# Bringing four rows of slots and weights to all partitions by way of DRAM instead of by products and evictions

## The reference

```python
def hier_moe(h, w_group, b_group, w_router, b_router, w_gate, w_up, w_down):
    """Two-level MoE: top-1 expert group, then top-2 experts inside that group."""
    ...
    top_v, top_i = lax.top_k(el_g, TOP_K_IN_GROUP)
    p_e = jax.nn.softmax(top_v, axis=-1) * p_g
    eidx = top_g[:, None] * EXP_PER_GROUP + top_i
    gates = (jax.nn.one_hot(eidx, N_EXPERTS, dtype=f32) * p_e[..., None]).sum(1).astype(x.dtype)
    y = jnp.zeros_like(x)
    for grp in range(N_GROUPS):
        sl = slice(grp * EXP_PER_GROUP, (grp + 1) * EXP_PER_GROUP)
        hg = jnp.einsum('td,edf->tef', x, w_gate[sl])
        hu = jnp.einsum('td,edf->tef', x, w_up[sl])
        act = jax.nn.silu(hg) * hu * gates[:, sl, None]
        y = y + jnp.einsum('tef,efd->td', act, w_down[sl])
```

## Time and profile before

| | us |
|---|---|
| median of 3 runs | 608.97 |
| lowest and highest | 608.93, 609.97 |
| the profiled execution, its own time | 609.4 |
| its span in the profile | 607.5 |
| mean granted clock of TensorE | 0.997 of full speed |

### The profile page before, as it was taken

One profiled execution on the slowest core, in us unless ns is written; L12 is line 12 of the kernel. 1 busy time (PEld: TensorE's weight loads), 2 busy tenths in 40 slices (PEclk: granted clock), 3 DMA queues, 4 the chain that ended last, 5 costly groups with the idle time before them and its releaser, 6 DMA issues.

```text
span 607.5 us, 8074 instructions
## 1 busy us (share of the span) xinstructions
PE 590.3 (97%) x3093; PEld 368.2 (61%) x3093; DVE 214.8 (35%) x625; ACT 146.6 (24%) x408; POOL 42.6 (7%) x87
## 2 busy tenths in 40 slices
PE   8999999999999999999998999999999899999996
PEld 4687878887664444444466777777777633333331
DVE  3352113420255444444464333333411542222222
ACT  3313123331321111111163333333311421111110
POOL 7010000000020000000003000000000111000000
PEclk9999999999999999999999999999999999999998
DMA  9979620126547999999997523120327598999971
GB/s 286 343 190 349 221 91 1 64 76 237 197 129 304 415 410 421 421 421 372 349 349 245 174 69 141 54 86 1 138 70 276 209 376 329 413 421 421 421 318 71
DMA packets 59124, 150.05 MB, mean 247 GB/s; under 512 B 10092, under 2 KB 42924, under 8 KB 46796
## 3 DMA queue, kind: packets, MB, share of 16 engines
q1 hardware_dynamic: 54992, 138.75, 61.2%
q0 software_dynamic: 2912, 10.64, 5.0%
q10 hardware_dynamic: 1180, 0.12, 0.2%
HBM read 146.27 MB, written 3.23 MB: 246 GB/s over the span
## 4 chain that ended last, share of the span: by engine, by line
PE 90%; DMA 5%; DVE 2%; ACT 1%; issue 1%; SPq 0%; DVEq 0%; POOLq 0%; ACTq 0%
PE bank L1395 36%; PE bank L1676 19%; PE bank L1704 9%; PE bank L1718 5%; PE bank L1647 3%; PE bank L1723 3%; PE bank L1506 1%; DMA qk_area<-xs,idx 1%; DMA ring<-in_m_w_in 1%; PE bank L1845 1%; PE bank L1889 1%; PE bank L1858 1%; PE bank L1885 1%; PE bank L1683 1%; DMA gate_area<-cs_dram 1%
## 5 line engine op out<-in xcount | busy, mean ns | idle before, releaser
L1395 PE MATMUL bank<-hxT,ring 128*128 128x272 f32 x576 | 138.2, 394 | 0.6 <-DVEq L1319 0.5
L1395 PEld LDWEIGHTS bank<-hxT,ring 128*128 128x128 f32 x576 | 107.8, 190 | 23.1 <-issue 2.1
L1676 PE MATMUL bank<-ring,gate_area 128*64 128x512 f32 x496 | 115.1, 597 | 0.0
L1676 PEld LDWEIGHTS bank<-ring,gate_area 128*64 128x64 f32 x496 | 34.5, 137 | 63.4 <-issue 62.6
L1395 PE MATMUL bank<-tok,ring 128*128 128x272 f32 (+1 forms) x256 | 59.6, 389 | 0.7 <-DVE tok L1372 0.6
L1704 PE MATMUL bank<-ring,gate_area 128*32 128x512 f32 (+1 forms) x368 | 58.0, 594 | 0.0
L1395 PEld LDWEIGHTS bank<-tok,ring 128*128 128x128 f32 x256 | 47.8, 190 | 11.8 <-issue 3.9
L1107 DVE TENSOR_TENSOR qk_area<-qk_area,bank 128x256 f32<-128x256 f32 x16 | 6.7, 422 | 92.6 <-ACT qk_area L754 92.6
L1704 PEld LDWEIGHTS bank<-ring,gate_area 128*32 128x32 f32 (+1 forms) x368 | 16.5, 119 | 36.2 <-issue 36.2
L538 POOL DMA_INDIRECT qk_area<-xs,idx x16 | 15.8, 987 | 311.7 <-DMA xs<-tok 199.4
L754 ACT ACTIVATE qk_area<-bank 128x256 f32<-128x256 f32 x16 | 6.2, 384 | 121.6 <-PE bank L1676 121.6
(11 more groups left out here) (302 smaller groups left out, 642.3 us busy)
## 6 DMA issues: line engine op xcount, KB each, us to landing
ring<-in_moe_w_gate SPq DMA_DIRECT2D x31, 1024.0 KB, 9.0
ring<-in_moe_w_up SPq DMA_DIRECT2D x31, 1024.0 KB, 10.8
ring<-in_moe_w_down SPq DMA_DIRECT2D x31, 1024.0 KB, 13.7
ring<-in_m_w_in SPq DMA_DIRECT2D x12, 1024.0 KB, 12.5
ring<-in_kv_w SPq DMA_DIRECT2D x8, 1024.0 KB, 12.4
ring<-in_m_w_out SPq DMA_DIRECT2D x4, 1024.0 KB, 12.9
ring<-in_f_w_q SPq DMA_DIRECT2D x4, 1024.0 KB, 12.0
ring<-in_f_w_o SPq DMA_DIRECT2D x4, 1024.0 KB, 6.6
```

Of the source, the lines that this page charges most:

```text
L1395: ins = pe.matmul(bank[c % 2][:, 0:n], w[:, k, half * P:half * P + P], x[:, k, 0:n], start=(k == 0), stop=(k == KB - 1))
L1676: ins = pe.matmul(bank[1][s, :], xgT[b % 2][:, q, s], unit_gate_up(us[par][0], q), start=(q == 0), stop=(q == KB - 1))
```

## The change

tokens_to_rows loses the second product of each tile. VectorE's copy to row4 takes 4 partitions instead of 36. ScalarE, behind xgT_evac(0) and ahead of silu(0), waits for row4 and issues a DMA that writes its four rows of n numbers to row4_dram. Where rows_spread made four evictions, ScalarE now waits for that write to have landed, and issues one DMA that reads the four rows back with a partition broadcast into bc4. combine_weights(0) waits for this DMA. The four products of spread_rows are gone, with their waits.

```diff
@@ build @@
+        row4_dram = nc.dram_tensor("row4_dram", [2, MH, NT], F32, kind="Internal").ap()
...
@@ LAYER0 @@
-                  1, "lg_read": 1, "bc_mm": 4, "bc_ready": 4, "xT_read": 8, ...
+                  1, "lg_read": 1, "bc_ready": 16, "xT_read": 8, ...
...
@@ ScalarE, moe(l) @@
                 def rows_spread():
 
-                    for r in range(4):
-                        act.wait_ge(*in_layer("bc_mm", l, r + 1))
-                        act.activation(bc4[:, r, 0:n], bank[4 + r][:, 0:n], ACT.Copy).then_inc(sem("bc_ready"), 1)
+                    act.wait_ge(sem("row4_out"), 16 * (l + 1))
+                    act.dma_start(bc4[:, :, 0:n], row4_dram[l, :, 0:n].partition_broadcast(P)).then_inc(sem("bc_ready"), 16)
...
                 xgT_evac(0)
+
+                act.wait_ge(*in_layer("row4_ready", l, 1))
+                act.dma_start(row4_dram[l, :, 0:n], row4[0:MH, 0:n]).then_inc(sem("row4_out"), 16)
                 for b in range(NPAIR):
                     silu(b)
...
@@ VectorE, moe(l) @@
                     if b == 0:
-                        dve.wait_ge(*in_layer("bc_ready", l, 4))
+                        dve.wait_ge(*in_layer("bc_ready", l, 16))
...
                 dve.wait_ge(*in_layer("row4_mm", l, 1))
-                dve.tensor_copy(row4[:, 0:n], bank[3][0:32 + MH, 0:n]).then_inc(sem("row4_ready"), 1)
+                dve.tensor_copy(row4[0:MH, 0:n], bank[3][0:MH, 0:n]).then_inc(sem("row4_ready"), 1)
...
@@ TensorE, moe(l) @@
                     for t, rows, c0 in tiles:
-                        pe.transpose(bank[3][0:MH, c0 - off:c0 - off + rows], tok4[0:rows, :, t], ident[0:rows, 0:rows])
-                        ins = pe.matmul(bank[3][32:32 + MH, c0 - off:c0 - off + rows], tok4[0:rows, :, t],
-                                        ident[0:rows, 0:rows], start=True, stop=True)
+                        ins = pe.transpose(bank[3][0:MH, c0 - off:c0 - off + rows], tok4[0:rows, :, t],
+                                           ident[0:rows, 0:rows])
                     ins.then_inc(sem("row4_mm"), 1)
-
-                def spread_rows(r0, r1):
-                    if r0 == 0:
-                        pe.wait_ge(*in_layer("row4_ready", l, 1))
-                        pe.wait_ge(*in_layer("xr_read", l, 1))
-                    for r in range(r0, r1):
-                        g = slice(32 * (r % 2), 32 * (r % 2) + MH)
-                        pe.matmul(bank[4 + r][:, 0:n], sel4[g, r, :], row4[g, 0:n], start=True, stop=True) \
-                            .then_inc(sem("bc_mm"), 1)
...
                     if b == 0:
                         rows_to_cols(1, 1)
-                        spread_rows(0, 2)
                         act_tr(0)
-                        spread_rows(2, 4)
                         continue
```

More of the change, by code:

```diff
@@ L284, in build @@
                   1, "rs_ffn": 1, "xr_tr": 6, "soft_in": 2, "soft_exp": 2, "xr_read":
-                  1, "lg_read": 1, "bc_mm": 4, "bc_ready": 4, "xT_read": 8, "xT_read0": 9, "gu_done": 8, "silu_done": 8,
+                  1, "lg_read": 1, "bc_ready": 16, "xT_read": 8, "xT_read0": 9, "gu_done": 8, "silu_done": 8,
                   "act_ready": 8, "down_done": 16, "y_read0": 8, "y_read1": 8, "eall_ready": 1, "pos_mm": 1,
```

## The result

| | before | after |
|---|---|---|
| median of 4 runs, us | 609.16 | 617.04 |
| lowest to highest, us | 608.93 to 609.97 | 616.64 to 617.5 |
| the profiled execution, us | 609.4 | 617.36 |

The ratio is 1.0127, 95% interval 1.0111 to 1.0143: 7.9 us slower. I had forecast 612.2 with a range up to 616.0. The direction was right, the size was not.

The account below looks back on a forecast made before the run. TensorE, busy for 97% of the span, was taken as the bound. Its gain of 2.1 us and late spreads of 1.8 and 3.5 us sum to +3.2, so 612.2 us after median adjustment, range 608.0 to 616.0.

Parts of the forecast that it names:

- Turning the tokens to rows, and the products: TensorE's path in both layers: removing L1618 and the four products gains 1.15 us in layer 0, 0.95 in layer 1.
- ScalarE costs nothing: ScalarE behind xgT_evac(1): the four evictions L738, 1.41 us, and the DMA issues in their place are worth nothing.
- Who waits: VectorE's combine_weights(0) waits for the rows; the idx copy behind it delays down(0). Allowed: 5.7 and 5.0 us to landing.
- Layer 0, 1.8 us late: Layer 0's spread: lands 7.5 us after issue against 5.7 allowed, so 1.8 us late, ends 0.6 and 3.3.
- Layer 1, 3.5 us late: Layer 1's spread: 512 packets land 8.5 us after issue, 3.5 us late, ends 0 and 6.0.
- the turns of one to one: DMA queues in layer 1: spread and loads alternate packet by packet; some 190 of 512 packets through until 504.3.
- rival D: DMA queues take turns in batches: layer 0 0.7 us late, layer 1 as forecast, 611.1 us; chance 0.10.
- rival E: TensorE's pause lowers its clock to 1.2 GHz: down(0) takes 3.65 us more in each layer, 619.5; chance 0.06.
- A: The forecast case, both layers' spreads late: 612.2 us, from 610.2 to 616.2 by the ends; chance 0.57.
- The sum: Whole kernel: -2.1 + 1.8 + 3.5 = +3.2 us on the profiled 609.4, so 612.6; forecast median 612.2.
- B: Both layers' spreads land in time, under 5.7 and 5.0 us: -2.1, 606.9 us; chance 0.15.
- C: Layer 0's spread in time, layer 1's late by about 2 us: 608.9, no change; chance 0.12.

Follow-up runs that it names:

- The last experiment: Changed kernel with layer 0's spread issued before silu(0), layer 1's in larger descriptors with its readers moved later: 608.58 us against 609.97 for the kernel before, ratio 0.9974.
- layer 0 alone: Changed kernel with only layer 0 spreading by DRAM, layer 1 keeping products and evictions: 610.05 us against 610.06 for the kernel before, ratio 1.0002.
- the larger descriptors: Changed kernel with layer 1's spread contiguous at both ends, 128 runs of 4 KB instead of 512 of 1 KB: 615.71 us, ratio 1.0096 to the kernel before.
- the kernel with the early issue: Changed kernel with the spread issued ahead of silu(0), once the write to DRAM has landed: 612.82 us against 609.71 for the kernel before, ratio 1.0052.

## Why the prediction was right and wrong

**Turning the tokens to rows, and the products.** Right. gate_up(1) starts 0.96 us earlier in layer 1 (forecast 0.95), and in layer 0 at 188.17 instead of 189.43; 0.13 of these 1.26 us the profile had gained earlier already, which leaves 1.13 (forecast 1.15). What was late next was VectorE's L1107 and L1114, as said. The last experiment shows most of the gain where nothing holds TensorE up behind it.

**ScalarE costs nothing.** Right for the engine. But the step that placed the issue was wrong: I let the queue issue the spread when ScalarE would have started its first L738, at 188.05 and 496.63. It was issued at 186.82 and 495.60, 1.2 and 1.0 us earlier, while evictions ahead of it were still to run. In layer 1 it was the write to DRAM that set the moment, which I had thought done long before: its packets moved from 494.57 to 495.18, and in every kernel here that spreads by DMA in layer 1 it goes out 0.3 to 0.8 us after the last of them.

**Who waits.** Right: the wait of combine_weights(0) held the idx copy and through it down(0), by one mechanism in both layers, and moving the readers took the loss away. I priced the way from landing to idx at 3.1 and 2.9 us; to down(0)'s start it is 3.5 (195.59 to 199.07) and 3.4 us (507.63 to 511.02). I had left out the start of VectorE behind the landing (0.10), that of the idx copy behind combine_weights (0.14) and that of TensorE behind the idx copy (0.14).

**Layer 0, 1.8 us late.** Measured 1.74, but by two errors that cancel. The landing took 8.8 us instead of 7.5, from an issue 1.2 us earlier, so it ended at 195.59 where I had 195.55. And the longer way to down(0) is offset by my reading of down(0)'s start: I took its weight load at 197.98, while its products start at 198.58 in the chain of before. Of the landing's 8.8 us the first packet takes 3.6, the packets 4.7 and the signal 0.5, where I had 3.9 for the packets and 3.6 for all the rest. (The free gather of 4.5 us, from which I took the upper end, stands in none of my rows; the chain of before has one of 4.36 us at 480.30.) Together with the 1.13 us gained that gives -1.13 + 1.74 = +0.6. rows_to_cols stands 0.71 later: down(0) itself takes 3.65 instead of 3.43 us behind its pause, and 0.13 had been gained before. Run against run, layer 0 alone costs -0.6 to +0.9 us.

**Layer 1, 3.5 us late.** This is the step that failed. I had 8.5 us to landing with an upper end of 11; it was 12.0 in the changed kernel's profile (11.1, 10.1 and 9.8 in the experiments that left the spread in its place). In terms: landing 3.5 us longer, issue 1.0 earlier, the way to down(0) 0.45 longer: 3.5 + 3.5 - 1.0 + 0.45 = 6.45, measured 6.44. In my own working it is the last term that was mis-sized. I let 190 packets through by 504.3, when I took the loads to be done, and gave the other 320 0.8 us on all 16 engines. In the trace 380 of the 512 are through by 504.3, twice as many, although the first of them came at 499.2, 3.6 us after the issue. But the other 132 take 2.9 us, to 507.2, since the last engine, as its packets' spacing shows, still took turns with the loads at 506. So the turns of one to one were right (47 and 48 packets in one window), and the end at 504.3 for all engines at once was wrong. Loads in front are behind both the late start and the long end: with them held back the first packet comes after 1.1 us and the landing after 6.4. Why one engine was so much later than the others was not followed.

**The turns of the queues (rival D).** The Trainium skill, DMA: Bandwidth & Descriptors, Queues, rings and completion order, has an engine drain a whole packet of 9 to 17 descriptors before it changes queues. The trace does not agree. The spread takes 39 to 55 packets per us beside 47 to 49 of the loads for three windows in a row, as even as the earlier trace rows. And the packets' start times show single turns: of the spread's 142 packets of 1 KB from 500 to 503, 125 have a packet of the loads starting 42 to 43 ns behind them and 18 one of the spread (10 to 20 would by chance); from 504.4 to 507.3, where the loads thin out, 117 of 128 have one of the spread. The late start could still be a backlog in a queue; no run separates that from a slow start of the DMA itself.

**The clock (rival E, 0.06).** It held, in layer 1 alone, on top of A, and I had given it too little. The Trainium skill, TensorE: Matmul & The Clock Gate, What's actually happening, says that idleness brings the gate down to 1.2 GHz. The profile agrees: 0.50 behind a pause of 6.44 us, and behind 4.51 (the larger descriptors); no fall behind 1.74 in layer 0. But the length of one pause does not settle it: in the kernel with the early issue it fell behind pauses of 1.65 and 0.56 us close together and not behind 2.96, and in the kernel before without L1618 it fell with no pause in any window. I had no row of a pause this long, and my own upper end of the stall, 6.0 us, should have carried the clock with it instead of leaving it a separate rival. The price was 2.13 us, not 3.65, because the clock came back before down(0) ended (0.07 of it is the pause's alone: down(0) takes 3.64 instead of 3.57 us behind 1.71 and 2.96 us of waiting at full clock).

**The sum.** Forecast -2.1 + 1.8 + 3.5 = +3.2; measured in these terms -2.1 + 1.7 + 6.4 + 2.1 = +8.1 against 7.9 in the runs. That the two meet so closely is in part luck: only layer 1's 7.6 us of it can be followed to the end, layer 0's +0.6 no longer shows at the start of layer 1, and the 0.5 us behind the last step has no cause here. 2.9 us of the miss is layer 1's stall, 2.1 the clock.

**The other rivals.** B (both in time) and C (layer 0 in time) are refuted by the two waits. B's 606.9 is also 0.4% under the kernel before; the best of my kernels, where TensorE never waits for the rows, came to 0.26%.

## What to carry to other kernels

A DMA that takes the place of engine work is priced by what the other queues hold at that moment as much as by its bytes (544 KB landed after 3.8 to 8.8 us here): look for the bulk loads issued just before it, and issue it ahead of them if its data is ready. On the engine that reads its result, put the reader behind every instruction that another engine is waiting for; here that order alone was worth the whole loss. And if the stall you forecast for TensorE can reach some microseconds, in one piece or in two, add the slower clock behind it to the same case.

## What the runs showed of the hardware that I had not expected

- ScalarE's queue issued a DMA (186.82) while three activations ahead of it in program order were still to run (from 187.07). In the kernel with the loads held back it came behind all four in layer 1 (497.22), because the last packet of the write that it waits for ended only at 496.89.
- Writing 4 KB to DRAM beside loads and gathers took 4.73 us (its first packet came after 3.7), longer than spreading 544 KB in the quiet stretch of the earlier trace rows.
- The granted clock fell while TensorE was busy in every window, behind four products that read only 4 partitions one after another (two pairs, 1.1 us each); with the same products on two groups of partitions, 0.63 and 0.66 us a pair, it stayed at 1.00. The second product of each tile, L1618, which looks like waste, saved more than it cost: taking it out alone made the kernel 0.35% slower.
